# Block 2's four late channel slices of the output projection move from the scan steps into the mixer

## The reference

```python
px = split_proj(modulate(x, pre_mix_g[l], mx[0], mx[1]) @ w_in[l])
ox, _, _ = hgrn_bidir(*hgrn_inputs(px, lb_f, lb_b), s_f, s_b)      # recurrence, 4 heads of 128 channels
a = hgrn_readout(o, p[4], onorm_g)                                 # 512 channels, slices 0 to 3
b = conv_branch(p[5], p[6], dw_w, dw_b, ln_g, ln_b, rows)          # 512 channels, slices 4 to 7
mix_x = jnp.concatenate([a, b], axis=-1) @ w_out
x = x + mx[2] * rms_norm(mix_x, post_mix_g[l])
hx = swiglu(modulate(x, pre_ffn_g[l], mx[3], mx[4]), ffn_w_gate[l], ffn_w_up[l], ffn_w_down[l])
x = x + mx[5] * rms_norm(hx, post_ffn_g[l])
```

## Time and profile before

| | |
|---|---|
| three runs | 1403.33, 1405.07, 1405.68 us |
| the profiled execution's own time | 1403.45 us |
| its span | 1401.7 us |
| PE matmul busy | 1353.7 us (97%) |
| DVE busy | 779.6 us (56%) |
| ACT busy | 382.5 us (27%) |
| POOL busy | 282.5 us (20%) |
| mean granted clock of TensorE, share of full | 0.991 |

### The profile page before, as it was taken

The page is one execution under the profiler, slowest core; times in us unless marked ns, Lnnn a source line. Parts: engine busy times, 40 slices in busy tenths (PEclk is TensorE's granted clock), DMA queues, the critical chain, the costliest instruction groups (busy, mean ns, idle before and its releaser), DMA issues. The chain is left out here.

```text
span 1401.7 us, 17536 instructions
## 1 busy us (share of the span) xinstructions
PE 1353.7 (97%) x6741; PEld 1132.6 (81%) x6741; DVE 779.6 (56%) x1001; ACT 382.5 (27%) x576; POOL 282.5 (20%) x123
## 2 busy tenths in 40 slices
PE   5899999999999988999999999999999999999998
PEld 2688888888888867888778888888888888888876
DVE  1798897889879797868554232314131423223237
ACT  3711321422132244746521111111111121211122
POOL 0522201211121100016342122121212212212110
PEclk9999999999999998999999999999999999999999
DMA  9461211120111020214252111111111120211132
GB/s 364 164 210 30 91 45 31 46 75 15 30 45 31 16 105 1 91 43 154 75 159 67 45 45 61 31 60 34 56 60 45 45 59 31 60 45 45 59 137 106
DMA packets 94716, 102.09 MB, mean 73 GB/s; under 512 B 3118, under 2 KB 77091, under 8 KB 94658
## 3 DMA queue, kind: packets, MB, share of 16 engines
q1 hardware_dynamic: 94658, 101.32, 21.7%
HBM read 92.92 MB, written 8.39 MB: 72 GB/s over the span
## 5 line engine op out<-in xcount | busy, mean ns | idle before, releaser
L1330 POOL TENSOR_TENSOR slot<-slotraw,slot 128x1024 fp32r<-128x1024 f32 x66 | 162.1, 2466 | 517.6 <-ACT slot L1263 304.6
L616 PE MATMUL bank<-h2Ta,slot 128*128 128x512 f32 x1056 | 245.7, 391 | 1.3 <-DVE mid L1882 1.3
L616 PE MATMUL bank<-slot,mid 128*128 128x512 f32 x1056 | 241.5, 389 | 2.8 <-POOL slot L1330 1.8
L616 PEld LDWEIGHTS bank<-slot,mid 128*128 128x128 f32 x1056 | 198.1, 188 | 44.6 <-POOL slot L1330 2.2
L616 PEld LDWEIGHTS bank<-h2Ta,slot 128*128 128x128 f32 x1056 | 198.9, 189 | 43.4 <-issue 2.1
L616 PE MATMUL bank<-cathi,slot 128*128 128x512 f32 x704 | 220.5, 389 | 0.0
L1544 DVE SCALAR_TENSOR_TENSOR cat<-conv_u,taps,cat 128x784 f32<-128x784 f32 (+29 forms) x120 | 158.1, 1317 | 9.5 <-DVE cat L1544 3.5
L616 PEld LDWEIGHTS bank<-cathi,slot 128*128 128x128 f32 x704 | 132.2, 188 | 27.7 <-issue 0.2
L616 PE MATMUL bank<-hT,ringb 128*128 128x512 f32 (+1 forms) x672 | 149.2, 378 | 0.0
L1904 DVE TENSOR_TENSOR arena<-bank,arena 128x512 f32<-128x512 f32 x144 | 99.5, 691 | 88.4 <-PE bank L616 87.8
L1879 DVE TENSOR_TENSOR mid<-bank,sgm 128x512 f32<-128x512 f32 x44 | 30.4, 690 | 202.3 <-ACT sgm L1278 202.3
(11 more groups left out here) (186 smaller groups left out, 1494.5 us busy)
## 6 DMA issues: line engine op xcount, KB each, us to landing
mraw<-in_w_mod SPq DMA_DIRECT2D x40, 512.0 KB, 7.0
slotraw<-in_ffn_w_gate SPq DMA_DIRECT2D x22, 512.0 KB, 3.7
slotraw<-in_ffn_w_up SPq DMA_DIRECT2D x22, 512.0 KB, 3.7
slotraw<-in_ffn_w_down SPq DMA_DIRECT2D x22, 512.0 KB, 4.2
ringinb<-in_w_in SPq DMA_DIRECT2D x12, 512.0 KB, 3.7
xst<-in_x SPq DMA_DIRECT2D x8, 512.0 KB, 12.9
ringina<-in_w_in SPq DMA_DIRECT2D x8, 512.0 KB, 4.6
ringinc<-in_w_in SPq DMA_DIRECT2D x8, 512.0 KB, 4.3
```

The lines of the kernel that those rows point to most:

```text
L616: return pe.matmul(o, l, r, start=start, stop=stop, skip_group_check=True)
L1330: return pool.tensor_tensor(lo, full, hi.bitcast(F32), ALU.subtract)
```

## The change

The "rest" units of block 2 are gone, and `mix(2)` multiplies all of slices 3 to 7. The four units left (blocks 0 and 1) are spread over the four steps 9, 10, 11 and 13, one in each. Before, the six units stood as two, two, one and one. DVE's list follows. The lines of the kernel after the change are 1 lower from L130 on, and up to 3 lower behind L1803.

```diff
-    _at += {9: [("rest", 0, 0), ("rest", 0, 1)], 10: [("rest", 1, 0), ("rest", 1, 1)],
-            11: [("rest", 2, 0)], OUT_AT + 1: [("rest", 2, 1)]}.get(_u, [])
+    _at += {9: [("rest", 0, 0)], 10: [("rest", 0, 1)], 11: [("rest", 1, 0)], OUT_AT + 1: [("rest", 1, 1)]}.get(_u, [])
...
-                ks = [3] if t < 3 else [3, 4, 5, 6, 7]
+                ks = [3] if t < 2 else [3, 4, 5, 6, 7]
...
                 elif u == 9:
                     rest(0, 0)
-                    rest(0, 1)
                     swish(1)
                 elif u == 10:
+                    rest(0, 1)
+                elif u == 11:
                     rest(1, 0)
+                elif u == OUT_AT + 1:
                     rest(1, 1)
-                elif u == 11:
-                    rest(2, 0)
-                elif u == OUT_AT + 1:
-                    rest(2, 1)
```

## The result

Over 20 runs of each, taken in turns, the changed kernel took 1407.95 us in the median (1402.81 to 1410.33), the kernel before 1403.57 us (1401.28 to 1405.68). The ratio is 1.0027, 95% interval 1.002 to 1.0033: 3.8 us slower, 2.8 to 4.6 (the two medians lie 4.4 us apart). The profiled execution of the changed kernel took 1406.84 us, with a span of 1405.1 us (before: 1403.45 and 1401.7).

What follows compares the result with a forecast made beforehand. The prediction took TensorE's row of matmuls, busy 1353.7 of 1401.7 us, as the bound. From a base of 1404.5 us, a new wait of +2.73 and the clock's fall of 1.5 gave 1408.7 us, range 1405.0 to 1410.6.

Steps and rivals of the forecast that it cites:

- The hole at step 9: Before the second group's "outer", PE waits 2.83 us for ACT's copies, where 0.10 was: 2.73 us lost.
- Step 10, "o", mixer: One unit fewer in step 10 wins 2.79 us: third "outer" at 595.85, "o" at 599.92, mixer at 614.96 us.
- The first turn: In the mixer, 24 more matmuls cost 5.58 us; the turn moves from 628.77 to 631.5, its input still covered.
- The fall of the clock: After step 9's new wait, at about 590 to 594 us, the clock falls to 0.50, costing 1.5 us.
- The sum: Whole kernel: the wait's 2.73 us plus the clock's fall, +4.23 us, giving 1408.7 from a base of 1404.5.
- Rival A: Step 9: the new wait without a fall of the clock, +2.73 us, 1407.2 us; chance 0.26.
- B: Step 9: the new wait and the clock's fall behind it, the forecast itself, 1408.7 us; chance 0.46.
- Rival D: Feed-forward start: 2.58 us wait and 1.57 of low clock vanish through DVE's lead; 1403.1 or 1400.4 us; chance 0.06.

Runs made afterwards that it cites:

- the kernel with six units: The kernel before with one unit moved from step 9 to step 10 (1, 3, 1, 1), mixer as before: 1407.91 us median of 12, ratio 1.0026.
- the one with the wait at "o": The changed kernel with its four units as 2, 1, 0, 1 in steps 9, 10, 11, 13: 1408.01 us median of 5, ratio 1.0034.
- the second profile: The changed kernel run once more with no edit, set beside the kernel before: 1409.36 us median of 5, ratio 1.0036.
- the filled hole: The changed kernel with the one unit of step 9 computed twice on PE, the result overwritten: 1405.70 us median of 11, ratio 1.0014.
- five units: The kernel before with units as 2, 1, 1, 1 in steps 9, 10, 11, 13, block 2's second half in the mixer: 1404.20 us, ratio 1.0003.

## Why the prediction was right

*The hole at step 9.* Predicted 2.73 us by the distance of ACT's copies from PE's end; measured 2.66 as a listed wait in three profiles and 2.82 by start times, where the prediction had 2.83, with ACT unmoved. The row without a listed wait was the one to read: the two units had covered the copies to within 0.1 us. Right, and shown by three kernels that open or move the hole.

*Step 10, "o", mixer.* Predicted 595.85, 599.92 and 614.96, measured 595.84, 599.91 and 614.95. The wait of 1.38 stayed. The first turn was to be 2.7 to 2.8 late and is 2.64.

*The fall of the clock.* Predicted at 1.5 us; where it came behind this wait it cost 1.40. But in the profiled execution it did not come, nor in that of the kernel with six units: of the three profiles with the wait at "outer" one shows it, and the one with the wait at "o" shows it too. By single execution that is two of four, less than "in most". It comes in some executions and not in others: one and the same kernel shows it in one profile and not in the other. The Trainium skill, page "TensorE: Matmul & The Clock Gate", Part 1, on the clock gate, calls the window in which the hardware watches activity free-running and says that the point of transition varies for that reason. The two profiles agree with this, and so does the scatter of the 20 runs, 1.9 us against 1.1 for before in the same turns; none of them shows the cause.

*The sum.* Forecast +4.23 us, measured +3.8 (2.8 to 4.6). The forecast of 1408.7 was 0.75 above the median of 1407.95, since I set the base at 1404.5 and it was 1403.6; the mean of the four times that I named is in truth 1404.4. Rival A alone, +2.73, lies below the interval, but by less than 0.1 us, and with the 0.76 us at 738 us it would be 3.5 and inside. So the changed kernel's time alone does not tell A from B. What speaks for a fall in a part of the runs is the second profile and the filled hole. The profiled execution is one of A in the scan steps: its rise of 3.4 us is made of 2.62 and 0.76, and not of 2.73 and 1.5. That the sum comes out so near it is in part luck.

*What was wrong.* Rival D's price. I counted 1.57 us for the fall of the clock at 683 us, and it is worth nothing there: behind it stands POOL's wait of 1.41, and 7.14 us go by with the fall or without. The wait itself could be removed, but by the order of the turns and not by a lead of DVE. And one term was missing: 0.76 us at 738 us, where a weight row landed late. Both profiles of the changed kernel have it (waits of 1.16 and 1.23 us), but there is only one profile of before to set against them, and how much of the median it makes is not shown. Nor did I count the wait of 1.81 us near 1360 us, behind which the clock falls in some executions at a cost of 1.6 us, in kernels with the hole and without it.

## What to carry to other kernels

Where fill work stands in front of a wait, measure its cover by the moment at which the input arrives on the other engine, and not by the list of waits: a wait of 0.1 us that is not even listed can be the one that decides, and the next unit taken away costs its full length. Work that only changes place on the busiest engine is free until the last cover is used up (five units: nothing that could be measured; four: 3.8 us), and the best place for a spare unit is an existing hole, as long as the other engines' chain behind it does not start later. Slow matmuls behind a hole may hide the next wait, so take a fall of the clock off the sum only after reading who else was late.

## What the hardware showed that I had not expected

Idle time on TensorE cost more than the same time filled with useless matmuls: 12 wasted matmuls in a hole of 2.7 us made the kernel 2.3 us faster in the median (1405.70 against 1407.95 us), with a mean granted clock of 0.9905 against 0.9890. The clock fell to 0.50 as early as within a wait of 2.66 us, and in other executions of the same wait it did not fall at all. Counted over the 13 profiles, it fell behind the wait of 2.66 us in 1 of 3, behind the wait of 2.6 us at the start of the feed-forward layer in 7 of the 9 that have it, and behind the wait of only 1.81 us near 1360 us in 7 of 13; behind the waits of 1.38 us ahead of the mixer it never fell.
